# Storing two convolution states element by element from the turned layout, in a hybrid decoder step

## What is computed

```python
def short_conv(u, buf, w):
    L = u.shape[1]
    full = jnp.concatenate([buf.astype(u.dtype), u], axis=1)
    y = w[0] * full[:, 0:L]
    for i in range(1, CONV_W):
        y = y + w[i] * full[:, i:i + L]
    return y, full[:, -(CONV_W - 1):]

def mixer(xn, pos, conv_buf, ret_state, w_in, conv_w, w_a, w_b, w_o):
    ...
    cb, cc, ch, q, k, v, g, ga, gb = jnp.split(proj, idx, axis=-1)
    conv_out, conv_new = short_conv(cc * ch, conv_buf, conv_w)
    o_a = jnp.einsum('blc,cd->bld', cb * conv_out, w_a)
    ...
    merged = jax.nn.sigmoid(ga) * o_a + jax.nn.sigmoid(gb) * o_b
    return jnp.einsum('bld,de->ble', merged, w_o), conv_new, ret_new
```

## Time and profile before

| | us |
|---|---|
| median of 3 runs | 1429.06 (1428.99 to 1429.4) |
| profiled execution, its time | 1430.51 |
| profiled execution, its span | 1428.4 |
| PE busy | 1355.8 (95%) |
| DVE busy | 387.2 (27%) |
| ACT busy | 252.3 (18%) |
| DMA, mean over the span | 364 GB/s |

### The profile page before, as it was taken

How to read it: one execution, slowest core, us unless ns; L and a number is a source line. 1 busy time by engine, 2 the same in 40 slices (tenths; PEclk the granted TensorE clock), 3 DMA queues, 4 the chain that set the end, 5 groups by cost and what they waited for, 6 DMA issues and landing times.

```text
span 1428.4 us, 17286 instructions
## 1 busy us (share of the span) xinstructions
PE 1355.8 (95%) x7193; PEld 706.2 (49%) x7193; DVE 387.2 (27%) x711; ACT 252.3 (18%) x375; POOL 94.1 (7%) x163
## 2 busy tenths in 40 slices
PE   8999999999999999999989989889899899998997
PEld 6667668788887543443323333333333333333342
DVE  4235443642501341321221112212121122111223
ACT  1233333321000431111111011111010111101112
POOL 1122213210000210000000000000000000000000
PEclk9999999999999999999999999999999999999999
DMA  9998879874433589999999999999999999999997
GB/s 349 366 312 283 302 251 337 288 265 159 151 129 154 207 372 428 432 433 427 434 430 433 433 429 434 429 433 433 429 435 429 432 433 430 434 430 430 428 426 287
DMA packets 42866, 519.94 MB, mean 364 GB/s; under 512 B 5146, under 2 KB 5706, under 8 KB 20900
## 3 DMA queue, kind: packets, MB, share of 16 engines
q1 hardware_dynamic: 28704, 471.67, 78.8%
q0 software_dynamic: 12576, 44.62, 9.1%
q10 hardware_dynamic: 1540, 2.99, 0.5%
HBM read 497.63 MB, written 21.67 MB: 364 GB/s over the span
## 4 chain that ended last, share of the span: by engine, by line
PE 70%; DMA 28%; DVE 1%; issue 0%; ACT 0%; SPq 0%; DVEq 0%; ACTq 0%
PE bank L1845 24%; PE bank L1532 23%; DMA arena<-in_w_pairs 16%; DMA ring<-in_w_pairs 12%; PE bank L1580 4%; PE bank L1810 4%; PE bank L1796 3%; PE bank L1894 2%; PE bank L1675 2%; PE bank L1549 1%; PE bank L1641 1%; PE bank L1843 1%; PE bank L1806 1%; PE bank L1874 1%; PE bank L1862 1%; PE bank L1583 1%
## 5 line engine op out<-in xcount | busy, mean ns | idle before, releaser
L1845 PE MATMUL bank<-ring,arena 128*64 128x512 f32 x1536 | 349.9, 608 | 35.1 <-DMA ring<-in_w_pairs 35.1
L1532 PE MATMUL bank<-arena,ring 128*128 128x264 f32 x1472 | 335.6, 388 | 0.0
L1532 PEld LDWEIGHTS bank<-arena,ring 128*128 128x128 f32 x1472 | 277.4, 190 | 52.1 <-issue 6.0
L1845 PEld LDWEIGHTS bank<-ring,arena 128*64 128x64 f32 x1536 | 112.8, 140 | 249.3 <-issue 229.6
L1894 PE MATMUL bank<-ring,arena 128*64 128x512 f32 x768 | 172.7, 595 | 4.0 <-DMA ring<-in_w_pairs 4.0
L1845 PE MATMUL bank<-arena 128*64 128x512 f32 x512 | 116.7, 603 | 11.1 <-DMA arena<-in_w_pairs 11.1
L1894 PEld LDWEIGHTS bank<-ring,arena 128*64 128x64 f32 x768 | 55.5, 137 | 102.0 <-issue 100.5
L1462 DVE TENSOR_SCALAR arena<-bank 128x512 f32<-128x512 f32 x32 | 22.1, 691 | 272.5 <-PE bank L1845 272.5
L1845 PEld LDWEIGHTS bank<-arena 128*64 128x64 f32 x512 | 36.5, 138 | 84.5 <-issue 84.5
L1481 DVE COPY arena<-bank 64x512 f32<-64x512 f32 x32 | 21.9, 683 | 184.0 <-PE bank L1894 184.0
L1452 DVE TENSOR_TENSOR hs<-hs,bank 128x256 f32<-128x256 f32 x16 | 6.7, 421 | 223.4 <-PE bank L1806 223.4
(11 more groups left out here) (241 smaller groups left out, 1013.1 us busy)
## 6 DMA issues: line engine op xcount, KB each, us to landing
ring<-in_w_pairs SPq DMA_DIRECT2D x59, 4096.0 KB, 28.9
arena<-in_w_pairs SPq DMA_DIRECT2D x19, 4096.0 KB, 27.9
ring<-in_w_mixer SPq DMA_DIRECT2D x58, 1024.0 KB, 8.6
ring<-in_w_pairs SPq DMA_DIRECT2D x26, 2048.0 KB, 12.9
arena<-in_w_pairs SPq DMA_DIRECT2D x9, 2048.0 KB, 17.3
arena<-in_state_ret POOLq DMA_DIRECT2D x32, 512.0 KB, 7.4
out_ret_sample<-arena POOLq DMA_DIRECT2D x32, 512.0 KB, 6.0
arena<-v_decode POOLq DMA_DIRECT2D x32, 256.0 KB, 6.9
```

The costliest lines, as they stand in the source:

```text
L1532: ins = pe.matmul(bank[:, 0:T], weight(n + k // 4, k % 4)[:, 128 * j:128 * (j + 1)], rhs[:, k, :], start=k == 0, stop=k == KD * groups - 1)
L1845: ins = pe.matmul(out, xgT[:, k, 64 * e:64 * (e + 1)], held(n, 2 * D * (k % W1_KS) + c), start=False, stop=k == KD - 1)
```

## The change

The event `ct` goes, with the four transposes on PE, ACT's copy and the two DMAs of rows. In its place an event `rows` stands directly behind `taps` of each half, with work on ACT alone: it waits until the four products of this half are in `U`, and issues eight DMAs out of `U` straight into the two outputs, four of 128 x 2 elements and four of 128 x 8. On the DRAM side neighbouring elements of one column of `U` are not next to each other for a partition, so each element of 4 bytes is a piece of its own. The semaphore `ctok_out` now counts sixteen DMAs. DVE waits for the first eight before it overwrites `U` with `ch` 1. `prepare_experts` on DVE and the first copy of `gb` 1 on ACT (which writes to `U`'s place) wait for all sixteen.

```diff
@@ mixer_order
-    turned = []
     for n, g in CONV_ORDER + (("ga", 0), ("cb", 1)):
         proj((n, g))
-        if turned:
-            main.insert(len(main) - 2, turned.pop())
         if n == "ch":
             main.append((("taps", g), 0.0))
-            turned.append((("ct", g), 0.5))
+            main.append((("rows", g), 0.0))
@@ bank_plan
-        elif what == "ct":
-            use(event, TURN_BANK)
@@ ScalarE
-                elif what == "ct":
-
-                    bank = read(ac, event)
-                    if h == 0:
-                        was_filled(ac, ("out", H - 1, 1))
-                        ac.wait_ge(saved, 32 * len(DEFERRED))
-                    empties(ac.activation(ctok[0:NS + 2, 512 * h:512 * (h + 1)], bank[0:NS + 2, :], ACT.Copy), event)
-                    if h == 1:
-                        for g in range(2):
-                            was_read(ac, ("ct", g))
-                        ac.dma_start(o["conv_prompt"][0, 0], ctok[0:2, :]).then_inc(ctok_out, 16)
-                        ac.dma_start(o["conv_sample"][0, :, 1, :], ctok[2:2 + NS, :]).then_inc(ctok_out, 16)
+                elif what == "rows":
+
+                    for j in range(4):
+                        was_read(ac, ("proj", ("ch", h), j))
+                    for j in range(4):
+                        c = slice(512 * h + 128 * j, 512 * h + 128 * (j + 1))
+                        ac.dma_start(o["conv_prompt"][0, 0][:, c].rearrange("r p -> p r"), U[:, j, LP:LP + 2], allow_slow_non_contiguous=True).then_inc(ctok_out, 16)
+                        ac.dma_start(o["conv_sample"][0, :, 1, c].rearrange("r p -> p r"), U[:, j, LP + 2:T + 2], allow_slow_non_contiguous=True).then_inc(ctok_out, 16)
...
+                        if (name, g, j) == ("gb", 1, 0):
+                            ac.wait_ge(ctok_out, 16 * 16)
@@ VectorE
-                v.wait_ge(ctok_out, 32)
+                v.wait_ge(ctok_out, 16 * 16)
...
-                            was_filled(v, ("ct", 0))
+                            v.wait_ge(ctok_out, 16 * 8)
@@ TensorE
-                elif what == "ct":
-                    g = which[0]
-                    bank = fill(pe, event)
-                    for j in range(4):
-                        was_read(pe, ("proj", ("ch", g), j))
-                    for j in range(4):
-                        ins = pe.transpose(bank[0:NS + 2, 128 * j:128 * (j + 1)], U[:, j, LP:T + 2], ident)
-                    fills(ins, event)
```

More of the change, by code:

```diff
@@ L396, in build @@
         aT = view(11880, KD, T)
-        ctok = view(14000, D)
         merged = view(6592, KD, T)
```

## The result

| | kernel before | kernel after |
|---|---|---|
| median, us | 1429.23 (1428.99 to 1430.38, 4 runs) | 1489.36 (1487.8 to 1499.06, 4 runs) |
| ratio to before, 95% interval | 1 | 1.0435 (1.0417 to 1.0453) |
| profiled execution: time and span | 1430.51 and 1428.4 | 1487.80 and 1485.6 |

The change costs 60 us. The forecast was 1435.6 us with a range to 1452. The sign and the place are right, and the size, 60 us against 6.5, is off by a factor of nine.

A forecast was written before the change was run, and what follows sets the result against it. PE was taken to set the pace through the mixer, up to about 500 us. Terms 5.2 + 0.2 + 1.7 - 0.9 gave +6.2, taken as +6.5 with bunched copies; 1429.06 + 6.5 = 1435.6 us, range 1427.5 to 1452.

The forecast's parts named there:

- What bounds the kernel: Up to about 500 us PE sets the pace; a microsecond at 250 to 320 us moves the expert stage one to one.
- The transposes' 0.88 us: Two groups of four transposes on PE's path in the mixer, 0.44 us each; removing them gains 0.88 us.
- ScalarE held: Issuing each half's stores holds ScalarE 12.5 and 9.5 us; PE waits 5.2 and 0.2; 1431 to 1450 us, chance 0.45.
- (a): Queue room counted in DMAs: eight fit, ScalarE's 3.5 to 5.4 us of issuing is covered; 1428.2 us, chance 0.30.
- (c): ScalarE held only briefly, the queue draining within the cover plus 3 us; 1428 to 1431 us, chance 0.08.
- The covers: Time ScalarE may be held after each half's product before PE must wait: 7.3 us first half, 9.3 us second.
- The size of a 4-byte packet: Each 4-byte DRAM write taken at 15 ns, range to 74; 3.4 and 3.5 us for the halves' remaining packets.
- The rule that spoke against the change: Skill guidance on the new stores: a strided last dimension becomes one descriptor per element and should be rearranged; floor near 10.5 ns.
- Room of 80 to 90 packets: ScalarE's queue takes about 80 to 90 packets per engine; a half's 328 don't fit, so the third or fourth DMA stands.
- Rival (b): All stores taken, but packets at 0.36 us land late; DVE stands at 289, PE from about 296; 1433 to 1446 us, chance 0.10.
- Rival (d): ScalarE held and each DRAM write 74 ns: PE waits 18.6 and 13.8 us, clock falls twice; about 1464 us, chance 0.05.
- The clock: A PE wait in the mixer can lower its granted clock; counted once at 1.7 us.

The follow-up runs named there:

- far stores: Kernel after with its sixteen stores still on ScalarE but into a DRAM scratch with neighbouring channels 512 bytes apart: 1437.45 us, ratio 1.0048.
- the spaced and the on-chip stages: Kernel before plus SyncE stages behind its last wait: four 4-byte-piece DMAs into DRAM 512 bytes apart, 7.1 us, or into on-chip memory, 4.6 us.
- the near stage: Kernel before plus a SyncE stage behind its last wait: four stores of 128x8 4-byte elements, 4 bytes apart in DRAM: 32.0 us.
- the near set of eight: Kernel before plus, behind its last wait, one half's eight stores issued by SyncE as in the change, neighbours 4 bytes apart: 35.9 us.
- the far set: Kernel before plus, behind its last wait, one half's eight stores issued by SyncE with 512 bytes between neighbours: 9.6 us.

## Why the prediction was right or wrong

**What bounds the kernel:** right. Waits, clock and transposes add up to the difference of the spans within 0.1 us, so a microsecond of PE in this stretch is a microsecond at the end.

**The transposes' 0.88 us:** in keeping with 1428.78 us without any stores and 1428.54 with DVE's, but never resolved.

**ScalarE held:** right that it happens and where, from the fourth issue on (6.38 us, against 1.27 for the third); the first `cc` 1 copy started past 262 us, as named. Cases (a) and (c), in which nothing or little is held, have fallen with it. The covers hold too. In after 28.5 us of hold less the 7.3 us of cover is 21.2, and PE waited 21.3; in the second half 22.2 less 9.3 is 12.9, and PE waited 13.6. With the far stores they hold once more: 13.0 less 7.3 is 5.7 against 5.83, and 10.7 less 9.3 is 1.4 against 1.32.

**The size of a 4-byte packet:** this step failed, and with it the number. It is the term 227 x 15 ns = 3.4 us (231 x 15 ns in the second half): ScalarE was to be free at 266.4, held 12.5 and 9.5 us, and was held 28.5 and 22.2. I took 15 ns and let the range reach 74, from the rates of 2 KB and 16 KB packets. Queue 10 in after holds 6.4% of 16 x 1485.6 us, 1521 us; less the 114 of before it is 1407 us for some 10,480 new packets, 134 ns each, nearly twice my upper end (the records of one engine overlap, so this is a packet's length and not an engine's time for it). The 15 ns were right for another kind of write: 20 and 11 ns in the two kernels with neighbours 512 and 64 bytes apart. Rows that show what bytes cost bound nothing about what a write costs that shares its line with fifteen others. No row of before has such a write, and I called 74 ns an end where there was none. The runs put a size to it: with neighbours 4 bytes apart and rows 4096 to 8192 bytes apart a store of 1024 elements takes 18 to 24 us, against 2.5 to 2.9 with neighbours 64 bytes or more apart.

**The rule that spoke against the change:** the Trainium skill (DMA: Bandwidth & Descriptors, Rules for kernel authors) says of a strided last dimension that it becomes one descriptor per element. The trace agrees: 12,016 packets. The floor of 10.5 ns a packet that the same page has under Measured, for loads issued from GpSimd, is near the 11 ns of the kernel with 64 bytes and lies under the spaced and the on-chip stages (7.1 and 4.6 us over 260 packets per engine, 27 and 18 ns with the latency in them); the near stage has 123 ns. That estimate strengthened me in a price for the wrong kind of write.

**Room of 80 to 90 packets:** wrong. 260 packets an engine were issued in 2.25 us with idle engines, and ten loads of 1 MB were not held either. The count gave the right place, the fourth issue, by luck. On idle engines the near set of eight was held at the fifth and seventh issue and the far set at none, so what drains slowly holds the issuer sooner. Where the limit lies was not found.

**Rival (b), out late:** half right, with the wrong victim. I had the wait before `ch` 1 late; in after DVE's first `ch` 1 product came at 333.61, right behind the decode step that had been late, and did not wait for a store. The victims were the decode states, whose store and load had to share the engines with the packets: 16.0 us of PE wait in after, and 49 when SyncE issued. I had counted the states as contention for the packets, put the reverse at nothing, and not asked what the packets do to the states. This is the second failed step: 16.0 of the 50.9 us of waits in after, and all of them once ScalarE isn't held. It too hangs on the dear packets: with neighbours 512 bytes apart PE waits 0.3 us for a decode step, and 3.7 with SyncE as issuer.

**Rival (d)** had the nearest number, 1464, at 0.05, and the two waits on ScalarE nearly right (18.6 and 13.8 us, measured 21.3 and 13.6). It has no decode state, and its 74 ns were an end of bytes, not a price of shared lines. **The clock** was counted once at 1.7 us; three long waits cost 7.1. So 5.2 + 0.2 + 1.7 - 0.9 of the forecast stand against 21.3 + 13.6 + 16.0 + 7.1 - 0.9.

## What to carry to other kernels

Before storing a turned tile element by element, look at where the elements of one DMA that belong to different partitions fall in DRAM: if they lie side by side, sixteen to 64 bytes, a store of 4 KB can take 20 us to land. The eight stores of one half (20 KB) took 36 us with nothing else running, and in the kernel they delayed the other streams' transfers. Cost a new DMA not only by what it delays on its issuer, but by each stream whose next step waits for a landing on the same engines. An element-wise store is easily replaced where an engine with idle time can turn the tile into longer pieces, 128 bytes here; then place the issue where the issuer has nothing queued behind it.

## What was new about the hardware

- 4096 elements of 4 bytes, 128 partitions on 16 engines, nothing else running: 32.0 us into DRAM with neighbours 4 bytes apart, 7.1 at 512 bytes, 4.6 into on-chip memory, 7.2 read from DRAM; as many pieces of 64 bytes 4.5.
- Inside the kernel, beside its other traffic: 134 ns a packet by queue 10's share with neighbours 4 bytes apart, 20 with 512, 11 with 64.
- A single store of the dear kind, alone: 18.8 us to landing, with the DMA engines busy for 2% of it.
- One store of 1024 elements by distance: 4 bytes 8.9 us, 32 bytes 3.5, 64 and more 2.5 to 2.9. By distance of its eight rows, at 4 bytes between neighbours: 512 bytes 8.9, 2048 14.6, 4096 23.6 (18.8 in another run), 4160 18.3, 8192 23.2. With neighbours 64 bytes apart, rows 8192 apart: 2.5.
- A single DMA issue held its engine for 39.26 us on SyncE and 16.8 on ScalarE, with everything behind it in that engine's stream.
